# Value projection of the second layer by seven block products, with its weight differences on POOL and four weight splits on DVE

## The reference

```python
def stick_breaking_attention(q, k, v): ...
def swiglu(x, w1, w3, w2):
    return (jax.nn.silu(x @ w1) * (x @ w3)) @ w2
# layer 1:
qc, kc, vc = jnp.split(h @ odd_w_in[o], 3, axis=-1)      # odd_w_in[o]: 1024 x 3072
mix = stick_breaking_attention(qc, kc, vc) @ odd_w_out[o]
h = layer_norm(DEEPNORM_ALPHA * h + mix, ln_mix_g[layer], ln_mix_b[layer])
```

## Time and profile before

| | us |
|---|---|
| median of 3 runs | 1157.35 (1156.26 to 1157.83) |
| the profiled execution's own time | 1156.23 |
| its span in the profile | 1154.5 |
| PE busy | 1133.9 (98% of the span) |
| DVE / ACT / POOL busy | 863.0 / 541.4 / 525.2 |
| value projection on PE | 562.84 to 608.18 |

### The profile page before, as it was taken

How to read it: one execution, slowest core, us unless ns; L and a number is a source line. 1 busy time by engine, 2 the same in 40 slices (tenths; PEclk the granted TensorE clock), 3 DMA queues, 4 the chain that set the end, 5 groups by cost and what they waited for, 6 DMA issues and landing times.

```text
span 1154.5 us, 19191 instructions
## 1 busy us (share of the span) xinstructions
PE 1133.9 (98%) x7461; PEld 988.1 (86%) x7461; DVE 863.0 (75%) x1202; ACT 541.4 (47%) x849; POOL 525.2 (45%) x346
## 2 busy tenths in 40 slices
PE   7999999999999999999999999999999999999997
PEld 6877768899999999888887777777999999998886
DVE  8558652897888888994804787866987888879957
ACT  6335665245444544553335555532545454454540
POOL 6897614356567773010353232203576666760000
PEclk9999999999999999999999999999999999999999
DMA  7623315143333336234243111202433333352341
GB/s 213 186 76 93 109 65 201 39 126 110 110 100 103 108 105 192 72 113 143 86 133 91 56 56 55 67 8 74 130 89 111 110 105 97 100 179 88 96 123 73
DMA packets 160186, 121.00 MB, mean 105 GB/s; under 512 B 19376, under 2 KB 140248, under 8 KB 160096
## 3 DMA queue, kind: packets, MB, share of 16 engines
q1 hardware_dynamic: 160096, 119.77, 34.7%
HBM read 116.32 MB, written 3.43 MB: 104 GB/s over the span
## 4 chain that ended last, share of the span: by engine, by line
PE 92%; DVE 5%; ACT 1%; POOL 1%; issue 1%; SPq 0%; DMA 0%; DVEq 0%; ACTq 0%; POOLq 0%
PE ps L2122 18%; PE ps L2124 17%; PE ps L2123 17%; PE ps L2154 5%; PE ps L2152 5%; PE ps L2153 5%; PE ps L2145 5%; PE ps L2147 5%; PE ps L2146 5%; PE ps L2661 2%; PE ps L2687 2%; PE ps L2672 2%; PE ps L2159 1%; PE ps L2705 1%; PE ps L2384 1%; PE ps L2707 1%
## 5 line engine op out<-in xcount | busy, mean ns | idle before, releaser
L848 POOL TENSOR_TENSOR wlo<-raw,whi 128x1024 fp32r<-128x1024 f32 x75 | 183.2, 2454 | 333.4 <-ACT whi L973 326.4
L2122 PE MATMUL ps<-xhi,whi 128*128 128x256 f32 (+1 forms) x848 | 272.1, 321 | 0.0
L2124 PE MATMUL ps<-xhi,wlo 128*128 128x256 f32 (+1 forms) x848 | 267.0, 315 | 0.0
L2123 PE MATMUL ps<-xlo,whi 128*128 128x256 f32 (+1 forms) x848 | 266.9, 315 | 0.0
L2122 PEld LDWEIGHTS ps<-xhi,whi 128*128 128x128 f32 x848 | 161.7, 191 | 17.6 <-issue 6.4
L927 POOL TENSOR_TENSOR wlo<-raw,whi 128x512 fp32r<-128x512 f32 x114 | 173.2, 1546 | 0.6 <-ACT whi L1235 0.4
L2124 PE MATMUL ps<-thi,wlo 128*128 128x256 f32 x608 | 172.2, 283 | 0.0
L2123 PE MATMUL ps<-tlo,whi 128*128 128x256 f32 x608 | 172.2, 283 | 0.0
L2122 PE MATMUL ps<-thi,whi 128*128 128x256 f32 x608 | 172.2, 283 | 0.0
L2124 PEld LDWEIGHTS ps<-xhi,wlo 128*128 128x128 f32 x848 | 161.8, 191 | 10.4
L2123 PEld LDWEIGHTS ps<-xlo,whi 128*128 128x128 f32 x848 | 161.9, 191 | 8.5
(11 more groups left out here) (293 smaller groups left out, 2355.6 us busy)
## 6 DMA issues: line engine op xcount, KB each, us to landing
raw<-in_ffn_w SPq DMA_DIRECT2D x126, 512.0 KB, 3.9
raw<-in_odd_w_in SPq DMA_DIRECT2D x24, 512.0 KB, 3.7
raw<-in_even_w_in SPq DMA_DIRECT2D x16, 512.0 KB, 4.5
t<-in_ffn_w SPq DMA_DIRECT2D x12, 512.0 KB, 6.4
h<-in_x SPq DMA_DIRECT2D x8, 512.0 KB, 5.0
raw<-in_even_w_out SPq DMA_DIRECT2D x8, 512.0 KB, 3.8
raw<-in_odd_w_out SPq DMA_DIRECT2D x8, 512.0 KB, 3.5
bias<-rel_scratch SPq DMA_DIRECT2D x8, 256.0 KB, 3.5
```

The lines of the kernel that those rows point to most:

```text
L848: eng.tensor_tensor(lo, raw_of(b), hi, ALU.subtract).then_inc(w_lo, 1)
L2122: eng.matmul(o_, w_hi_, x_hi_, start=start, stop=False)
L2123: eng.matmul(o_, w_hi_, x_lo_, start=False, stop=False)
L2124: return eng.matmul(o_, w_lo_, x_hi_, start=False, stop=stop)
```

## The change

The product is formed from 2x2 blocks with seven block products in place of eight. X11, X12 are the first 256 tokens' first and second 512 features, X21, X22 those of the last 256 tokens; W11 to W22 are the quarters of the matrix. With the differences of weights `v1` = W12 - W11, `v2` = W22 - v1, `v3` = W22 - W12, `v4` = W21 - v2, and sums of x `S7` = X11 - X21, `S6` = X22 - S7, `S5` = S6 + X11, `S3` = X12 - S6, the products are P1 = X11 W11, P2 = X12 W21, P4 = X22 v4, P7 = S7 v3, P6 = S6 v2, P5 = S5 v1, P3 = S3 W22. Each product has two parts (halves of its 512 inner features), each a unit of 128x1024 weights: 14 units (`V_UNITS`) of 12 matmuls 128x512. The eight copies of PSUM at the end become one copy on ACT and 14 adds of 128x512 on DVE (`v_add`), which form the four blocks of `ov` out of the products.

New work: POOL forms 8 differences of 128x1024 (`v_sums`), two of them in the stage before; POOL splits units 1 to 10, DVE the last four (`v_lower`); DVE forms four sums of x (`s_full`) and their low parts (`s_lower`), ACT their high parts (`s_upper`); ACT keeps the first 256 tokens of x in `xf` and the product P1 in `sg`. SP loads the right half of the matrix directly into `v1`, `v2` (`load_right_columns`, 4 transfers of 512 KB) before the blocks of the stage; six units come through `raw`. The matrix's lower right quarter is loaded twice.

```diff
@@ -174,8 +174,15 @@
 
     ffn_blocks(0)
     OV = len(load_of)
-    for k in range(KT):
-        row_tiles(owi, k * P, 2 * D, D)
+    V_UNITS = [(p, part) for p in (P1, P2, P4, P7, P6, P5, P3) for part in range(2)]
+    V_END = OV + len(V_UNITS)
+    V_SUMS = [(P7, 0), (P7, 1), (P5, 0), (P6, 0), (P5, 1), (P6, 1), (P4, 0), (P4, 1)]
+    for p, part in V_UNITS:
+        if p in (P1, P2, P3):
+            k0 = 2 * part + (0 if p == P1 else KT // 2)
+            row_tiles(owi, k0 * P, 2 * D + S * (p == P3), S)
+        else:
+            load_of.append(None)
...
+                    if OV <= last < V_END and V_UNITS[last - OV][0] != P3:
+                        p, part = V_UNITS[last - OV]
+                        sp_.wait_ge(v_sum, v_sum_upto(P5 if p == P1 else P4, part))
...
+                    if b == out_end(0) - 1:
+                        load_right_columns()
+
+            def load_right_columns():
+                sp_.wait_ge(joint_lo, GS)
+                for part in range(2):
+                    for k0, p in ((0, P5), (KT // 2, P6)):
+                        eng.dma_start(v_store(p, part), tiles_of(owi, (k0 + 2 * part) * P, 2 * D + S, S, 2)).then_inc(
+                            right_landed[part], 16)
...
+            def v_sums(p, part):
+                upper, lower = (raw[:, raw_slot(v_block(q, part)), :].rearrange("p (k n) -> p k n", k=2) for q in (P1, P2))
+                t1_, t2_, t3_, t4_ = (v_store(q, part) for q in (P5, P6, P7, P4))
+                if p == P7:
+                    pool.wait_ge(right_landed[part], 32)
+                    pool.wait_ge(w_used, ordinary(out_first(0) + max(
+                        u for u, unit in enumerate(UNITS[0]) if unit[0] == HALF1) + 1))
+                    o_, a, b_ = t3_, t2_, t1_
+                if p == P5:
+                    pool.wait_ge(*landed(v_block(P1, part)))
+                    pool.wait_ge(v_sum, v_sum_upto(P7, part))
+                    o_, a, b_ = t1_, t1_, upper
+                if p == P6:
+                    pool.wait_ge(v_sum, v_sum_upto(P5, part))
+                    o_, a, b_ = t2_, t2_, t1_
+                if p == P4:
+                    pool.wait_ge(*landed(v_block(P2, part)))
+                    pool.wait_ge(v_sum, v_sum_upto(P6, part))
+                    o_, a, b_ = t4_, lower, t2_
+                eng.tensor_tensor(o_, a, b_, ALU.subtract).then_inc(v_sum, 1)
+
+            v_sums(P7, 0)
+            v_sums(P7, 1)
             pool.wait_ge(w_lo, ordinary(out_end(0)))
-            norm(1, OV)
+            lower_upto(OV + 1)
+            for p, part in V_SUMS[2:]:
+                v_sums(p, part)
+            lower_upto(v_block(P5, 0))
+            split[0] = V_END
+            pool.wait_ge(w_lo, ordinary(V_END))
             lower_upto(OQK + LEAD + 4)
...
+                def keep_x(t):
+                    act.wait_ge(x_ready, NT * (n + 1) + t + 1)
+                    eng.copy(xf[:, :, t * P:(t + 1) * P],
+                             psf[:, 2 * t * S:2 * t * S + D].rearrange("p (k n) -> p k n", k=KT)).then_inc(xf_ready, 1)
...
                 for t in range(NT - 1):
                     if n < 3 and t == 2:
                         upper_x(n + 1, 0)
+                        if n == 1:
+                            keep_x(0)
                         upper_x(n + 1, 1)
                     std(t)
                 upper_upto(f + 3)
+                if n == 1:
+                    keep_x(1)
+                    keep_first(0)
                 std(NT - 1)
-                if n < 3:
+                if n == 1:
+                    keep_first(1)
+                    upper_x(2, 2)
+                    upper_upto(f + 4)
+                    upper_x(2, 3)
+                elif n < 3:
                     upper_upto(f + 4)
                     upper_x(n + 1, 2)
                     upper_x(n + 1, 3)
...
+            def keep_first(t):
+                if t == 0:
+                    act.wait_ge(v_first, 1)
+                else:
+                    act.wait_ge(w_used, v_used(P1))
+                eng.copy(sg[:, t, :], ps[:, V_BANK[P1] + t, :]).then_inc(v_kept, 1)
...
+            def s_upper(p):
+                act.wait_ge(s_sum, S_ORDER.index(p) + 1)
+                if p == P3:
+                    act.wait_ge(w_used, v_used(P7))
+                eng.copy(s_part(s_hi, p), s_full[:, S_ORDER.index(p) % 2]).then_inc(s_rounded, 1)
...
             norm(1, OV)
-            for k in range(KT):
-                upper_upto(OV + k)
+            upper_upto(v_block(P7, 0))
+            s_upper(P7)
+            s_upper(P6)
+            upper_upto(v_block(P7, 1))
+            act.wait_ge(w_used, v_used(P2))
+            eng.copy(ov[:, 0:2, 0:S], ps[:, V_BANK[P2]:V_BANK[P2] + 2, :]).then_inc(ov_out, 1)
+            upper_upto(v_block(P6, 0))
+            s_upper(P5)
+            upper_upto(v_block(P5, 0))
+            s_upper(P3)
             upper_upto(OQK + 3)
-            for i, t in enumerate(OV_ORDER):
-                if i < NT - 1:
-                    act.wait_ge(ov_done, i + 1)
-                else:
-                    act.wait_ge(w_used, ordinary(OV + KT))
-                eng.copy(ov[:, t, :], psf[:, 2 * t * S:2 * (t + 1) * S]).then_inc(ov_out, 1)
...
+            def s_lower(p):
+                dve.wait_ge(s_rounded, S_ORDER.index(p) + 1)
+                tt(s_part(s_lo, p), s_full[:, S_ORDER.index(p) % 2], s_part(s_hi, p).bitcast(F32),
+                   ALU.subtract).then_inc(s_lowered, 1)
+
+            def v_add(o_, a, p, t, op=ALU.add):
+                if p in V_FIRST and t == 0:
+                    dve.wait_ge(v_first, V_FIRST.index(p) + 1)
+                else:
+                    dve.wait_ge(w_used, v_used(p))
+                tt(o_, a, ps[:, V_BANK[p] + t, :], op).then_inc(v_added, 1)
+
+            def own_adds(p, t):
+                dve.wait_ge(v_added, v_added_upto(p, t))
...
+            dve.wait_ge(xf_ready, 2)
+            tt(s_of(0), first_rows(0).rearrange("p k (t n) -> p k t n", t=2), rows_late(0), ALU.subtract).then_inc(s_sum, 1)
+            dve.wait_ge(s_sum, 1)
+            tt(s_of(1), rows_late(KT // 2), s_of(0), ALU.subtract).then_inc(s_sum, 1)
+            s_lower(P7)
+            s_lower(P6)
+            dve.wait_ge(s_sum, 2)
+            dve.wait_ge(s_lowered, 1)
+            tt(s_full[:, 0], s_full[:, 1], first_rows(0), ALU.add).then_inc(s_sum, 1)
+            dve.wait_ge(v_kept, 2)
+            for t in range(2):
+                v_add(v_of(2 + t, 0), sg[:, t, :], P4, t)
+            s_lower(P5)
+            dve.wait_ge(s_sum, 3)
+            dve.wait_ge(s_lowered, 2)
+            tt(s_full[:, 1], first_rows(KT // 2), s_full[:, 1], ALU.subtract).then_inc(s_sum, 1)
+            def v_lower(p, part):
+                b = v_block(p, part)
+                dve.wait_ge(w_hi, ordinary(b + 1))
+                dve.wait_ge(w_lo, ordinary(b))
+                tt(wlo[:, slot(b), :], source_of(b), whi[:, slot(b), :].bitcast(F32), ALU.subtract).then_inc(w_lo, 1)
+
+            for t in range(2):
+                v_add(v_of(t, 1), sg[:, t, :], P7, t, ALU.subtract)
+            v_lower(P5, 0)
+            s_lower(P3)
+            v_lower(P5, 1)
+            for t in range(2):
+                own_adds(P7, t)
+                v_add(v_of(t, 1), v_of(t, 1), P6, t)
+                own_adds(P4, t)
+                v_add(v_of(2 + t, 0), v_of(2 + t, 0), P6, t)
+                v_add(v_of(2 + t, 1), sg[:, t, :], P6, t)
+            v_lower(P3, 0)
+            v_lower(P3, 1)
+            for t in range(2):
+                own_adds(P6, t)
+                v_add(v_of(2 + t, 1), v_of(2 + t, 1), P5, t)
+            for t in range(2):
+                v_add(v_of(t, 1), v_of(t, 1), P3, t)
...
-            def v_part(k):
+            def v_unit(p, part):
                 def run(half):
-                    if half == 0:
-                        pe.wait_ge(w_lo, ordinary(OV + k + 1))
-                    for t in (2 * half, 2 * half + 1):
-                        mm = token_rows(OV + k, k, 0, D, xhi, xlo, t, 2 * t, 2, k == 0, k == KT - 1)
                     if half:
-                        mm.then_inc(w_used, 1)
+                        return
+                    b = v_block(p, part)
+                    pe.wait_ge(w_lo, ordinary(b + 1))
+                    if p == P1:
+                        pe.wait_ge(xf_ready, 1)
+                    if p == P4:
+                        pe.wait_ge(xf_ready, 2)
+                    if p == P5:
+                        pe.wait_ge(s_sum, 2)
+                    if p == P7:
+                        pe.wait_ge(ov_out, 1)
+                    if p in S_ORDER:
+                        pe.wait_ge(s_lowered, S_ORDER.index(p) + 1)
+                    for t in range(2):
+                        if p == P2:
+                            pe.wait_ge(v_kept, t + 1)
+                        if p in (P6, P3):
+                            pe.wait_ge(v_added, v_added_upto(P7 if p == P6 else P5, t))
```

(29 more changed lines are left out.)

60 lines of the change are left out of this document (52 added, 8 removed).

## The result

The changed kernel takes 1161.76 us (median of 5 runs, 1160.33 to 1163.94); the kernel before, on the same chip, 1156.26 (1155.81 to 1157.83). The ratio is 1.0043, 95% interval 1.0028 to 1.0059: about 5 us slower, where +4.0 us, to 1161.3, was forecast. The profiled execution took 1163.94 us, the longest of the five, its span 1161.2.

What follows compares the result with a forecast made beforehand. PE, busy 98% of the span, was taken to bound the kernel. Removed matmuls, stand and slower clock, -5.44 + 7.5 + 1.9 = +4.0 us, took 1157.35 to 1161.3 us; range 1156.4 to 1164.2, some 0.85.

Steps and rivals of the forecast that it cites:

- What is removed: Value stage on PE: 168 matmuls in place of 192, 24 x 0.2267 = 5.44 us less, all on the path.
- The stand: PE in front of unit P6: waits 7.5 us for DVE's first add of P7.
- written order: Value stage: timed list of DVE, POOL and ACT instructions, with P7's first add ending at 593.8.
- The rule of turns: DVE with two SBUF inputs and POOL alternate; the waiting one goes next, ahead of a follower on the same engine.
- shorter chain: Rival before P6: DVE's fourth sum precedes POOL's split, PE stands 5.3 us; 1157.8 to 1159.7 us, chance 0.17.
- DVE first each time: Rival: DVE keeps its turn, stands of 1.7 at P7, 1.7 at P6, 1.3 at P3; 1156.6 us, chance 0.05.
- no collision: Rival in the value stage: DVE and POOL take no turns, no wait is left; 1151.9 us, chance 0.10.
- The clock: PE's granted clock falls in the stand before P6, costing 1.9 us, bounds 0 and 3.7.
- Hidden terms: POOL's differences, late splits, SP's extra transfers and ACT's copies of x: 0 us, up to 2.4 if one is late.
- at P3 I found no wait: Behind P6: no other PE wait, DVE's four splits written by about 604, P3 due at 604.7.
- The sum: Whole kernel: removed matmuls, stand and slower clock give +4.0 us, median to 1161.3 us, 0.34% slower.
- the base that the forecast used: Median time of the kernel before, taken as 1157.35 us.

Runs made afterwards that it cites:

- e7: Kernel before with 24 of its 192 value-stage matmuls left out, nothing else changed: 1152.52 us, ratio 0.9961.
- e5: Changed kernel with all fourteen splits on POOL and DVE's four splits gone: 1161.03 us, ratio 1.0030.
- e6: Changed kernel with POOL's eight weight differences cut to 4 of 512 columns of each tile: 1162.19 us, ratio 1.0036.
- e1: Changed kernel with the last three sums and a copy of the first in PSUM, one SBUF input per sum or low part: 1153.19 us, ratio 0.9968.
- e2: Changed kernel with three POOL splits (P7's second part, both of P6) cut to 8 of 1024 columns: 1153.65 us, ratio 0.9969.
- e3: Changed kernel with 26 unused matmuls added on PE between P7's end and the wait before P6: 1159.66 us, ratio 1.0025.
- e4: Changed kernel with DVE's adds of P4 and P7 ahead of later sums, ACT casting P6's second part before S5: 1158.75 us, ratio 1.0007.
- e11: e1 with P5 and P6 swapped, DVE's P3 splits ahead of its P5 and P6 adds, ACT's cast of P5's first part earlier: 1152.34 us, 0.9963.
- e8: e1 with units P5 and P6 swapped, POOL splitting P5 and DVE P6: 1160.42 us, ratio 1.0019.

## Why the prediction was right

**What is removed** (-5.44): -5.44 (e7).

**The stand** (7.5): 7.19 us of wait in the trace, 7.35 from the gap (596.13 - 588.55, less the usual 0.23). Up to PE's restart, each step of the written order that the rows show came within 0.1 us. The low part of S6 ended at 586.44, forecast 584.2 + 2.24; the third sum at 589.77 against 587.5 + 2.24; the fourth at 595.39 against 593.2 + 2.24. PE started P6 31.05 us after the stage's start, forecast 31.06. The rule of turns from the earlier trace rows carried this: POOL's split at 591.87 went ahead of the fourth sum, as the order of asking said, and the shorter chain, which hung on that, did not come. The margin was 0.15 us; e5 and e6 have the same 7.19 us, so it held in three profiles; that the forecast kept a chance of 0.17 for the other order was right with a margin so small. DVE first each time, and no collision, are excluded by the same rows. That it is the second SBUF input was argued from durations in the forecast; e1 and e2 show it.

**The clock** (1.9, bounds 0 and 3.7): 2.3 us. Eleven matmuls from 596.13 to 600.93 took 4.80 us instead of 2.49. With PE kept at work 2.1 to 2.2 us came back (e3). The low level outlasted the restart by 4.8 us, and about half of that is the loss. That the fall comes was read rightly from the earlier trace rows, and e4, with 3.3 us without work, agrees; in the changed kernel it came 5 us after the last matmul. The size is in part luck. After the same stand, e5 lost 2.9 us and e6 1.7, so no single value could be forecast. And the earlier trace rows don't show what I took from them: by their own numbers the sixteen transposes lost 16 x (0.228 - 0.136) = 1.5 us, not 1.9, and the granted clock was 1.00 there, not the lower level. The window of the kernel before that holds them:

```profile
5.00:10.00 5.00, 3.65 (x16) 3.28 (x16) 4.69 (x16) 2.63 (x5) 0.80 (x1) 1.00 1.01 353
```

Why they were slow stays open.

**Hidden terms** (0): e6 confirms it for the differences, e5 for DVE's splits. e11 confirms it for all of them together, loads and copies too: it carries all the new work and has the ratio 0.9963, where e7, which has none of it, has 0.9961. They were not without effect. In the stage before, DVE's split took 2.47 us beside POOL's difference instead of 1.22, and PE shows no wait for it. DVE in the changed kernel:

```profile
537.39 2.47 DVE L1561 TENSOR_TENSOR wlo<-raw,whi 128x1024 fp32r<-128x1024 f32 x1 [3.61 <-ACT whi L1404]
```

**What I missed**: at P3 I found no wait. There are 0.19 us in the trace, 0.4 with the restart. I followed DVE up to its splits of P3, done at about 604, and compared them with P3, due at 604.7. The add of P5 stands behind those splits, and P3 needs that too. In the trace the splits end at 608.92 and the add starts at 608.85, though P5's first tile was done at 608.13 (607.74 + 0.39). The splits were also 2.7 us later than 604 + 2.24, behind adds of P6 that waited for the slower PE. One reading was wrong as well: of DVE's 39.2 us of idle time only 32.9 lie in the stage, the rest behind it. Nothing was worked out from it.

**The sum** was -5.44 + 7.5 + 1.9 = +4.0. The stage grew by 4.80: -5.44 + 7.35 + 2.31 + 0.42, and 0.16 of smaller gaps. The median, at 1161.76, is 0.5 us over the forecast, and this closeness is in part luck: the kernel before came out at 1156.26, 1.1 us under the base that the forecast used, and against it the change is +5.0 by the ratio and +5.5 by the medians, not +4.0. The span shows the same miss, 1161.2 where 1158.5 was forecast: 4.80 from the stage, 2.24 from the first 42 us, -0.34 behind the stage.

## What to carry to other kernels

Before giving an idle DVE new work beside a busy POOL, count the tensor inputs that each new instruction takes from SBUF. With two it takes turns with POOL's, and 1.2 us become up to 3.4; with one of them in PSUM it costs its own length, and here that exchange turned 0.4% slower into 0.3 to 0.45% faster. Then write down the order of both engines in time, and look for the short instruction that PE needs behind the long ones: idle time in sum says nothing about it. And price a stand of PE with its slower restart, as a range: here one of 3.3 us cost 1.6 us more, and one of 7.2 us 1.7 to 2.9.

## What the runs showed of the hardware that I had not expected

- The clock can fall after PE is back at work: in e4 PE stood from 600.9 to 604.2, worked at full speed for 0.8 us, and then had 0.50 in the windows from 605 to 608; in e8 it was back at 604.3 and the clock fell some 0.5 us later.
- What the fall costs hardly follows the stand's length: 1.6 us for a stand of 3.3 (e4) and for one of 4.8 (e8), and 1.7, 2.3 and 2.9 us for three of 7.19 (e6, the changed kernel, e5). The fall itself came from about 3 us (e5) to 5 us (the changed kernel, e8) after PE's last matmul.
- The busy time of PE hides such a loss: in the stage it is 42.76 us, where the same matmuls take 39.90 in e11. That the page's total is as before, 1133.8 us with 24 matmuls fewer against 1133.9, is half this and half the slower start of this one profile. The mean clock (0.994, before 0.998), the windows and the distance between matmuls tell it.
